# Six norm borders in one fused program: part of VectorE's work goes to GpSimd and ScalarE, the normed operand is made two blocks at a time, and the statistics stand elsewhere in TensorE's order

## What is computed

```python
# first block
h = rms_norm(x) * (1 + sc1) + sh1
u, v, z, xbc, dt, gate_a, gate_b = split(h @ w_in)
mixed = sigmoid(gate_a) * (sgu(u, v) @ w_gm) + sigmoid(gate_b) * (ssd(z, xbc, dt) @ w_ssm)
x = x + g1 * (mixed @ w_out)
h2 = rms_norm(x) * (1 + sc2) + sh2
x = x + g2 * (square(relu(h2 @ w_ff1)) @ w_ff2)
x = rms_norm(x, final_norm_w)
# second block: two layers, the mixer is attention in the first, a pool mixer in the second
for i in range(2):
    x = layer_norm(ALPHA * x + 0.5 * swiglu(x, gu[i, 0], down[i, 0]))
    x = layer_norm(ALPHA * x + mixer_i(x))
    x = layer_norm(ALPHA * x + 0.5 * swiglu(x, gu[i, 1], down[i, 1]))
```

## Time and profile before

| | |
|---|---|
| device time, median of 3 runs (lowest, highest) | 1518.98 us (1518.51, 1521.5) |
| the profiled execution: device time, span in the profile | 1525.12 us, 1522.8 us |
| mean granted clock of PE in it | 0.989 |
| busy: PE, DVE, ACT, POOL | 1475.5, 1114.7, 839.3, 184.6 us |

### The profile page before, as it was taken

How to read it: one execution, slowest core, us unless ns; L and a number is a source line. 1 busy time by engine, 2 the same in 40 slices (tenths; PEclk the granted TensorE clock), 3 DMA queues, 4 the chain that set the end, 5 groups by cost and what they waited for, 6 DMA issues and landing times.

```text
span 1522.8 us, 25731 instructions
## 1 busy us (share of the span) xinstructions
PE 1475.5 (97%) x10189; PEld 1365.3 (90%) x10189; DVE 1114.7 (73%) x1474; ACT 839.3 (55%) x1135; POOL 184.6 (12%) x169
## 2 busy tenths in 40 slices
PE   8999998999999999999989989999999999899997
PEld 7999998889888899888989988889888898888887
DVE  7788987887877758666586697665966659886655
ACT  5655567655555446555454565554665545565543
POOL 0120003562000010000130020001300013030001
PEclk9999999999999999999999999999999999999999
DMA  8957756646445654555534335555455553445550
GB/s 328 370 212 277 262 203 228 216 150 215 191 173 202 239 219 169 191 193 193 193 132 176 137 119 213 193 194 192 146 202 196 186 186 136 152 182 195 191 194 28
DMA packets 43401, 295.94 MB, mean 194 GB/s; under 512 B 5052, under 2 KB 7228, under 8 KB 8750
## 3 DMA queue, kind: packets, MB, share of 16 engines
q1 hardware_dynamic: 40574, 280.24, 50.7%
q0 software_dynamic: 2736, 14.41, 2.7%
HBM read 291.44 MB, written 3.19 MB: 193 GB/s over the span
## 4 chain that ended last, share of the span: by engine, by line
PE 55%; DVE 7%; ACT 2%; issue 1%; DMA 0%; ACTq 0%; DVEq 0%
PE banks L708 24%; PE banks L710 12%; PE banks L723 5%; PE banks L725 4%; PE banks L726 4%; DVE w_lo L1868 2%; DVE part L1963 1%; ACT w_hi L1298 1%; DVE pw L2612 0%; DVE XS L2122 0%; PE banks L795 0%; PE banks L794 0%; PE banks L796 0%; DVE XS L1945 0%; PE banks L1205 0%
## 5 line engine op out<-in xcount | busy, mean ns | idle before, releaser
L1868 DVE TENSOR_TENSOR w_lo<-raw,w_hi 128x1024 fp32r<-128x1024 f32 x490 | 613.0, 1270 | 279.4 <-ACT w_hi L1298 275.4
L1298 ACT ACTIVATE w_hi<-raw 128x1024 fp32r<-128x1024 f32 x490 | 508.6, 1055 | 366.1 <-PE banks L710 176.9
L708 PE MATMUL banks<-H,w_hi 128*128 128x512 f32 x1504 | 522.2, 392 | 1.9 <-DVE w_lo L1868 1.9
L710 PE MATMUL banks<-H,w_lo 128*128 128x256 f32 x1504 | 420.4, 280 | 0.0
L708 PEld LDWEIGHTS banks<-H,w_hi 128*128 128x128 f32 x1504 | 282.3, 188 | 64.9 <-DVE w_lo L1868 2.8
L710 PEld LDWEIGHTS banks<-H,w_lo 128*128 128x128 f32 x1504 | 282.4, 188 | 0.0
L708 PE MATMUL banks<-HH,w_hi 128*128 128x512 f32 x480 | 166.8, 392 | 1.8 <-DVE w_lo L1868 1.8
L891 PE MATMUL banks<-H,w_lo 128*128 128x256 f32 x512 | 146.2, 286 | 2.0 <-ACT gate_a L1538 2.0
L893 PE MATMUL banks<-H,w_hi 128*128 128x256 f32 x512 | 144.1, 282 | 0.0
L894 PE MATMUL banks<-H,w_hi 128*128 128x256 f32 x512 | 144.1, 281 | 0.0
L723 PE MATMUL banks<-HH,w_lo 128*128 128x256 f32 x480 | 134.3, 280 | 0.0
(11 more groups left out here) (369 smaller groups left out, 2605.4 us busy)
## 6 DMA issues: line engine op xcount, KB each, us to landing
raw<-in_panels SPq DMA_DIRECT2D x265, 1024.0 KB, 4.8
rows<-cum_rows POOLq DMA_DIRECT2D x16, 384.0 KB, 4.6
late_w<-in_panels POOLq DMA_DIRECT2D x4, 1024.0 KB, 5.1
bias_rows<-rev POOLq DMA_DIRECT2D x1, 2048.0 KB, 11.4
XS<-in_x_t SPq DMA_DIRECT2D x4, 256.0 KB, 5.3
near<-bias_rows POOLq DMA_DIRECT2D x8, 128.0 KB, 3.4
out_t<-XS SPq DMA_DIRECT2D x4, 256.0 KB, 2.6
ws<-in_ws_t POOLq DMA_DIRECT2D x1, 512.0 KB, 11.3
```

Source lines behind the costliest of these rows:

```text
L708: pe.matmul(bank, w_hi[:, panel_slot, at:at + P], operand[:, kk, :, :].rearrange("p a t -> p (a t)"), start=starts and c == chunks[0], sto ...
L710: return pe.matmul(bank[:, 0:T], w_lo[:, panel_slot, at:at + P], operand[:, kk, 0, :], start=False, stop=stops and c == chunks[-1])
L1298: act.activation(w_hi[:, sl, w], raw[:, r, w], ACT.Copy).then_inc(panel_hi, 1)
L1868: vec.tensor_tensor(w_lo[:, sl, w], raw[:, r, w], w_hi[:, sl, w], ALU.subtract).then_inc(panel_lo, 1)
```

## The change

It touches the six borders, and ff2.

1. The statistics' matmuls stand behind another block k of the unscaled group: 3 (out, pool_out), 4 (att_out), 1 (the others, as before).
2. At out, att_out and pool_out POOL makes the first three adds of `part`, which DVE made.
3. `low_half`: POOL makes `w_lo` of the first half of the unscaled group's second panel (128 x 1024). DVE made it, behind its last add of `part`.
4. `mean_off`: POOL adds minus the mean to x at centred borders, in four instructions of 128 x 512.
5. DVE scales, and makes the low part, two blocks at a time (4 + 4 instructions of 128 x 512 for 8 + 8 of 128 x 256). It multiplies by the root alone; ACT applies the column weight and the bias, and writes the full x as well as the high part: 16 instructions for 8. POOL's bias adds behind these borders go.
6. The first group is taken up by a multiplication and one add of 128 x 1024. What is added (mean and bias) ACT makes in four instructions ahead of `next_half(0)`. qk's bias on ACT behind `first_scaled` goes.
7. ff2 takes in the late panels at every other panel, not at four in a row.

```diff
+STATS_BEHIND = {"out": 3, "ff2": 1, "down0": 1, "att_out": 4, "down1": 1, "pool_out": 3}
+SUMMED_BY_POOL = {name: BANKS + (name in SUMMED_AHEAD) for name in NORMED}
...
+            def low_half(name):
+
+                q = FIRST_PANEL[INDEX[name] + 1] - 1 + SPLIT
+                r, slot, _ = raw_place(q)
+                pool.wait_ge(panel_hi, 2 * q + 1)
+                pool.wait_ge(panel_lo, 2 * q)
+                pool.tensor_tensor(w_lo[:, slot, 0:PANEL // 2], raw[:, r, 0:PANEL // 2], w_hi[:, slot, 0:PANEL // 2], ALU.subtract)\
+                    .then_inc(panel_lo, 1)
+
+            def mean_off(i):
+
+                name = CENTRED[i]
+                pool.wait_ge(S["mean_kept"], [n for n in UNSCALED_ORDER if n in CENTRED].index(name) + 1)
+                pool.wait_ge(S["unscaled_lo"], unscaled_count(name, KD - 1))
+                away = st[:, 0, :].unsqueeze(1).to_broadcast([P, 2, T])
+                for a in range(KD // 2):
+                    two = slice(2 * a, 2 * a + 2)
+                    pool.tensor_tensor(xb[:, two, :], xb[:, two, :], away, ALU.add).then_inc(S["norm_centred"], 2)
...
-                        last.then_inc(half_used, 1)
-                        if p == 0 and half == 0:
-                            whole_stats(stage)
+                                if b == BANKS - 1 and c % 2:
+                                    last.then_inc(half_used, 1)
+                            if k == STATS_BEHIND[stage]:
+                                whole_stats(stage)
...
-                            ins = act.activation(H[:, m, 0, :], src[:, m, :], ACT.Identity, bias=bias[:, m:m + 1])
-                        ins.then_inc(S["norm_hi"], 1)
+                            hi = act.activation(H[:, m, 0, :], src[:, m, :], ACT.Identity, bias=bias[:, m:m + 1],
+                                                scale=scale[:, m:m + 1])
+                            full = act.activation(src[:, m, :], src[:, m, :], ACT.Identity, bias=bias[:, m:m + 1],
+                                                  scale=scale[:, m:m + 1])
...
+                    if stage_name in CENTRED:
+                        act.wait_ge(S["edges_kept"], edges_count(stage_name))
+                        for b in range(BANKS):
+                            act.activation(ev[:, 1 - G, b, :], st[:, 3, :], ACT.Identity, bias=edges[:, b, 1:2],
+                                           scale=edges[:, b, 0:1]).then_inc(S["shift_ready"], 1)
                     rest(s, G, lambda half: split(q + SPLIT, *raw_place(q + SPLIT), halves=(half,)))
...
-                split_after(split, name, 0)
                 unscaled_lo(name, KD - 1)
...
+                    vec.wait_ge(panel_lo, 2 * (q - 1) + 1)
                     split_after(split, stage_name, 1)
+                    vec.wait_ge(S["stat_root"], n + 1)
+                    for a in range(KD // 2 + 1):
+                        if a < KD // 2:
+                            scaled(a)
+                        if a:
+                            lo(a - 1)
+                        if a < KD // 2:
+                            split_half(q + a // 2, a % 2)
...
+                    vec.tensor_tensor(first, group_banks(G), root, ALU.mult).then_inc(taken, 1)
                     if mean:
+                        vec.wait_ge(S["shift_ready"], BANKS * ([n for n in UNSCALED_ORDER if n in CENTRED].index(stage_name) + 1))
                         vec.wait_ge(taken, FIRST_GROUP[s] + 1)
-                        vec.tensor_tensor(first, first, root, ALU.mult).then_inc(S["first_scaled"], 1)
+                        vec.tensor_tensor(first, first, ev[:, 1 - G, :, :], ALU.add).then_inc(S["first_scaled"], 1)
...
-                if 0 <= late < LATE:
-                    mod_panel(MODS_IN_GATES + late)
+                if 0 <= late < 2 * LATE and late % 2 == 0:
+                    mod_panel(MODS_IN_GATES + late // 2)
```

## The result

The changed kernel takes 1542.03 us (median of 4 runs, 1538.25 to 1543.01) against 1520.24 us of the kernel before in the same runs: 21.8 us slower, ratio 1.0139 (95% interval 1.0116 to 1.0162). The forecast was slower, but by 5.3 us, and the time lies outside its range.

What follows compares the result with a forecast made beforehand. PE, busy 97%, bounds the kernel, so only its waits and clock matter. Terms 6.2 + 0.6 + 3.6 + 1.9 - 4.5 - 1.7 - 0.5 - 0.3 = +5.3 us, on median 1518.98: 1524.3 us, range 1511 to 1533.

Steps and rivals of the forecast that it cites:

- The lock: POOL and DVE, both reading two SBUF inputs, do not share: about 1.1 us per 128x512 add, 2.05 for low_half.
- 2.2 us: At ff2, down0 and down1: PE's wait for the sums with low_half on POOL; +6.2 us for three.
- What stands behind the statistics: Chain from statistics to third group's half, 22.6 us, unchanged (bounds -2.5, +2.5); waits of 2.9 stay at att_out, 1.5 at pool_out.
- the slow clock, which was to swallow 3.1 us of the wait: At att_out and pool_out: slow clock stretches PE's work by 3.1 us, swallowing as much of waits of 6.0 and 4.6.
- the -0.5 at down1: Down1 to gu2: wait of 1.72 us shrinks to about 1.2 although PE comes 2 us later.
- shorter middle against longer end: Chain behind the statistics: half as many scalings and low parts, mean off DVE, against +1.2 us at the end.
- beside DVE's chain, which is the longer: ACT's eight more instructions a border cost nothing; if not, 3.4 us a border would show.
- The mean on POOL: At centred borders: spares DVE two passes of the kind of 1.23 us; four POOL instructions of 1.1 to 1.3 in the way.
- The clock at ff2, down0 and down1: Rival: clock falls behind their 2.2 us waits, +4 to +8 us, 1528 to 1532; chance 0.17, shared with the table-load rival.
- att_out: Border att_out: +3.6 us, 0.7 more first wait than today's 4.55 and 2.9 of wait behind the statistics.
- qk: Third group at qk: the 4.5 us wait goes (-4.5), and the slow clock behind it (-1.7).
- Late panels: At ff2: the 1.83 us wait before the second panel goes, 1.5 comes: -0.3 us, bounds -1.8 and +0.8.

Runs made afterwards that it cites:

- the run with the old end: First group's end as before, against the kernel with low half and mean on DVE and statistics behind k = 1: 1520.48 us, 1.0011 of before.
- the new end: Changed kernel with low half and mean back on DVE and statistics behind k = 1 at all six borders: 1528.72 us.
- the run with qk's edit alone: Kernel before, with ScalarE rounding qk's third-group first half ahead of its biases: 1515.34 us, 0.9967 of before.

## Why the prediction was wrong

The lock was right, and so was its price in waits. Timelines of POOL and then DVE at down1 in the changed kernel: POOL takes the half while the adds run, and DVE's three adds take 4.24 us for 2.14.

```profile
1079.69 2.37 POOL L695 TENSOR_TENSOR w_lo<-raw,w_hi 128x1024 fp32r<-128x1024 f32 x1 [2.49 <-ACT w_hi L1333]
```

```profile
1079.10 4.24 DVE L1999 TENSOR_TENSOR part<-part,XS 128x512 f32<-128x512 f32 x3
```

The 2.37 us are those of the earlier trace rows, and 2.10 us of delay stand for the 2.05 forecast. The waits of 2.29 (twice) and 2.35 us above are the "2.2 us" forecast.

What the forecast had for each border, and what the two profiled executions show (us; the last column is PE's waits from the border's first unscaled matmul to the third group, before and after):

| | forecast | measured | waits |
|---|---|---|---|
| out | +0.6 | -0.4 | 3.4, 2.9 |
| between out and ff2 (late panels) | -0.3 | +2.3 | |
| ff2 | +2.05 | +3.6 | 0.3, 2.4 |
| down0, with qk | 2.05 - 6.2 = -4.15 | -1.7 | 4.7, 3.0 |
| att_out | +3.6 | +7.8 | 4.7, 10.3 |
| down1 | 2.05 - 0.5 = +1.55 | +4.2 | 1.9, 4.5 |
| pool_out | +1.9 | +4.4 | 3.0, 7.9 |
| sum | +5.3 | +20.2 | 18.0, 31.0 |

Where it failed:

- **"What stands behind the statistics ... I take it as unchanged"** (the chain to the third group's half) is the step that failed. At down1 the chain ran from 1083.39 to 1106.80 + 1.23 = 1108.03, 24.6 us for the 22.6 before; from the statistics to the third group's start it is 24.9 us at att_out, 24.7 at down1 and 25.1 at pool_out. That is inside the bounds given for this term, but it counts at three borders. PE's waits behind the statistics are 2.08 + 3.06 = 5.1 us at att_out where 2.9 was forecast, 2.08 + 3.05 = 5.1 at pool_out where 1.5 was, and 2.24 at gu2 where 1.2 was: 6.8 us in all. Of the 15 us between 5.3 and 20.2 these waits are the largest part, and the clock at ff2, down0 and down1 (below) is the next. At pool_out one more reason is that the slow clock, which was to swallow 3.1 us of the wait, took only 1.7 (0.76 in 7 us). And the -0.5 at down1 had no ground: chain and PE's work both start at the statistics, so that PE comes 2 us later covers nothing. At down1 the first part of the chain was 18.4 us again (to 1101.78), as taken; its end 6.25 for the 4.2 before, where I had 5.4. The rows, DVE and then ScalarE:

```profile
1101.09 0.69 DVE L2150 TENSOR_TENSOR H<-XS,H 128x512 fp32r<-128x512 f32 x1 [0.82 <-ACT XS L1467]
...
1104.34 1.23 DVE L2182 TENSOR_TENSOR ev<-ev 128x1024 f32<-128x1024 f32 x1 [1.02 <-ACT ev L1475]
1106.80 1.23 DVE L1904 TENSOR_TENSOR w_lo<-raw,w_hi 128x1024 fp32r<-128x1024 f32 x1 [1.23 <-ACT w_hi L1333]
```

```profile
1102.23 2.08 ACT L1475 ACTIVATE ev<-st,edges 128x256 f32<-128x256 f32 x4 [1.24 <-DVE edges L2176]
1104.33 1.28 ACT L1413 ACT_TABLE_LOAD   x1
```

The shifts start 0.45 us behind the last low part, since they wait for the `edges` that DVE copies after it, and take 2.08 us, not the 1.70 of qk's biases. Then table load, half and low part follow one another, as listed. The trade "shorter middle against longer end" did not come: at three borders it is 2 us each, shown by the run with the old end (1.05 for 3.13).
- **The middle was hardly shorter** because ScalarE paces it: a pair of blocks is one half (0.95 in step) and four activations (0.49), 2.9 us, so 11.6 for four, and DVE's waits of 0.21 and 0.81 for ACT in the run with the mean on DVE are its sign. At down1 the stretch from ScalarE's first rounding to the last low part is 11.6 us for 12.4 before, and the first rounding comes 0.7 us later behind the statistics (6.8 for 6.0, from start times), so nothing is left. The prediction had ScalarE's instructions "beside DVE's chain, which is the longer", and had 3.4 us a border if not. Each takes 0.59 us, where the eight before took 0.51 (one line's instructions at this border after, and before, ns min/median/max):

```profile
L1465 ACT ACTIVATE H<-XS,cols x8: 582/587/602, 1090.2 to 1099.9; 128x256 fp32r<-128x256 f32 x8
```

```profile
L1430 ACT ACTIVATE H<-XS,cols x8: 489/510/511, 1079.8 to 1091.2; 128x256 fp32r<-128x256 f32 x8
```

  The Trainium skill, "ScalarE: Activation LUTs", section "What ACT_TABLE_LOAD costs", gives 186 ns + 0.833 N ns for an activation and some 93 ns more for each operand that is a pointer to a column. An estimate from this page is 0.585 us for 256 columns with bias and scale as columns, and 0.49 with one of them. The trace agrees with both (medians 0.587 and 0.510), and the page would have given the price beforehand.
- **The mean on POOL** was priced at 1.1 to 1.3 a piece; it took 6.49 us for four, and DVE's instructions beside it 2.30 and 1.78 instead of 1.22 and 0.69:

```profile
1084.77 6.49 POOL L706 TENSOR_TENSOR XS<-XS,st 128x512 f32<-128x512 f32 x4 [2.71 <-ACT st L1446]
```

```profile
1086.12 2.30 DVE L1904 TENSOR_TENSOR w_lo<-raw,w_hi 128x1024 fp32r<-128x1024 f32 x1
1088.34 1.78 DVE L2141 TENSOR_TENSOR XS<-XS,st 128x512 f32<-128x512 f32 x1
```

  That it was worth little in time (nothing that shows, with the low half undone) agrees with ScalarE being the pace behind it.
- **The clock at ff2, down0 and down1** stood in the sum at nothing and among the rivals at +4 to +8. In the profiled execution it came, 1.7 us at each, 5.1 in all.
- **att_out:** 7.8 for 3.6. The first waits were sized right: 3.53 + 1.63 = 5.2 us for the 4.55 + 0.7 forecast. What was not are those behind, as above. The border's time up to the third group, the slow clock in it included, takes the change apart: 31.0 us before and 32.9 with the adds alone; then 32.3 in the run with the old end, 34.4 with the new end, 37.6 with the later statistics too, 38.0 with the mean on POOL too, and 37.2 with the low half too, which is the changed kernel. So the adds on `U_early`, the new end and the later statistics (whose cover ahead is taken away behind, as the prediction had it) do it. The low half, which costs 1.9 us at this border alone on the kernel before, adds nothing once the statistics stand behind k = 4.
- **qk** was right: 4.5 to 0.70 us, and a simpler edit of the same kind, alone on the kernel before, gives 5.2 us for the 6.2 forecast (4.5 + 1.7).
- **Late panels** -0.3: measured 0.0 alone; one wait went, as forecast, and one came, of 1.79 us for the 1.5 priced, and at ff2's last part. In the changed kernel the slow clock follows that wait (last section), which makes 1.7 of the 2.3 us between out and ff2.

In sum, by the ratios: the changed kernel is 21.1 us over before. Undoing one part after another leaves 12.0 (low half), 9.9 (mean too), 5.8 (statistics behind k = 1 too) and 1.7 us (old end too). What is then left agrees with the parts that were added to the kernel before: 4.0 for the adds, some -3 for two blocks, 0 for the late panels. So some 9 us are the low half, 4 the later statistics, 4 the first group's new end (net of its gain at qk) and 4 the adds with DVE's new order; two blocks take 3 off. Each of these steps is uncertain by 2 to 5 us, and the mean's 2 us are within that. What stays open is the clock within single steps: it differs from one execution to the next, and no run here holds it still.

## What to carry to other kernels

Work moved from VectorE to an idle GpSimd was not moved off VectorE's path here, where both read two operands from SBUF: its price was nearly GpSimd's duration (2.1 us for a half of 2.4), paid wherever VectorE's next such instruction was late already. Before moving a piece, ask what stands between the last instruction of the chain and the first that the bound engine waits for: shifts ahead of a table load cost 2 us more at three borders than the fused instructions they replaced, while the same rearrangement gained 2 us at qk, the one border without the load, and a much smaller edit gained 5 there. Statistics moved further behind took off one wait and brought back others where the chain behind them had no slack.

## What the runs showed of the hardware

The same wait is followed by the slow clock in one execution and not in another. Out's wait of 3.44 us was followed by a clock of 0.56 before; in the run with qk's edit alone the same wait of 3.44 us was not:

```profile
395.80 0.48 PE L809 MATMUL banks<-part,mean_w 128*128 128x256 f32 x1 [3.44 <-DVE part L1966]
```

```profile
392.00:403.00 11.00, 7.57 (x62) 7.31 (x61) 10.28 (x18) 7.63 (x13) 0.00 (x0) 1.00 0.33 121
```

With the low half alone on POOL, ff2's wait of 2.40 us was followed by 1.00 and down0's 2.29 by 0.76:

```profile
579.00:586.00 7.00, 4.60 (x37) 4.34 (x37) 6.13 (x8) 3.55 (x7) 2.01 (x1) 1.00 0.13 25
766.00:773.00 7.00, 4.71 (x23) 4.13 (x22) 5.23 (x6) 2.54 (x6) 1.84 (x1) 0.76 0.00 0
```

The wait of 1.79 us ahead of ff2's last part was followed by 0.76 in the changed kernel and by 1.00 in the run with the late panels alone:

```profile
544.00:551.00 7.00, 7.00 (x48) 7.00 (x48) 6.39 (x8) 2.00 (x3) 0.32 (x1) 0.76 0.51 171
```

```profile
544.00:551.00 7.00, 7.00 (x62) 7.00 (x62) 6.62 (x9) 2.13 (x2) 0.00 (x0) 1.00 0.60 205
```

So behind waits of 1.8 to 3.4 us the slow clock took between 0 and 3 us, which is also the size of the spread between runs of one kernel.
